# Splitting a weight unit in one pass instead of two on GpSimd

## The reference

```python
proj = xn @ w_in                 # 1024 x 3072, 1024 x 5632, 2816 x 1024, ...
x = x + (b * u) @ w_out
x = x + (jax.nn.silu(a) * g) @ w_down
...
merged = jax.nn.sigmoid(gate_a) * y_gla + jax.nn.sigmoid(gate_b) * y_swa
x = x + merged @ w_out[l]
```

## Time and profile before

| | |
|---|---|
| median of 3 runs | 2173.0 us (2172.61 to 2173.7) |
| the profiled execution | 2173.7 us, its span 2171.9 us |
| TensorE matmul busy (PE) | 98% of the span |
| GpSimd busy (POOL) | 69% |
| VectorE busy (DVE) | 45% |
| ScalarE busy (ACT) | 20% |
| instructions of GpSimd | 1615 |
| bytes moved | 193.44 MB, mean 89 GB/s |
| mean granted TensorE clock | 0.997 of full |

### The profile page before, as it was taken

How to read it: one execution, slowest core, us unless ns; L and a number is a source line. 1 busy time by engine, 2 the same in 40 slices (tenths; PEclk the granted TensorE clock), 3 DMA queues, 4 the chain that set the end, 5 groups by cost and what they waited for, 6 DMA issues and landing times.

```text
span 2171.9 us, 30026 instructions
## 1 busy us (share of the span) xinstructions
PE 2122.8 (98%) x10839; PEld 1771.5 (82%) x10847; DVE 981.3 (45%) x1527; ACT 428.9 (20%) x871; POOL 1503.2 (69%) x1615
## 2 busy tenths in 40 slices
PE   5999999999999999999999999999999999999999
PEld 4888888888798887888888888888877888888887
DVE  5555655531446666675541156345744243222201
ACT  2002111100334434211100053222223112111000
POOL 4878888867764445798877846445544777777674
PEclk9999999999999999999999999999999999999999
DMA  4333333323333221333323322223222333333232
GB/s 125 97 106 107 90 96 96 93 81 99 104 103 83 78 78 49 103 107 98 96 75 97 112 75 70 77 59 88 59 72 65 88 98 97 97 97 97 80 90 82
DMA packets 366903, 193.44 MB, mean 89 GB/s; under 512 B 6512, under 2 KB 363216, under 8 KB 366816
## 3 DMA queue, kind: packets, MB, share of 16 engines
q1 hardware_dynamic: 363168, 186.67, 30.1%
q10 hardware_dynamic: 3648, 5.59, 0.8%
HBM read 190.11 MB, written 2.13 MB: 89 GB/s over the span
## 4 chain that ended last, share of the span: by engine, by line
PE 93%; DVE 4%; ACT 1%; issue 1%; ACTq 0%; DMA 0%; DVEq 0%
PE PS L482 22%; PE PS L484 22%; PE PS L483 22%; PE PS L745 2%; PE PS L729 2%; PE PS L630 2%; PE PS L731 2%; PE PS L730 2%; PE PS L746 2%; PE PS L747 2%; PE PS L632 2%; PE PS L631 2%; PE PS L546 1%; PE PS L577 1%; PE PS L814 1%; PE PS L952 1%
## 5 line engine op out<-in xcount | busy, mean ns | idle before, releaser
L465 POOL TENSOR_TENSOR RING<-RAW,RING 128x512 fp32r<-128x512 f32 x708 | 966.2, 1365 | 59.0
L462 POOL TENSOR_SCALAR RING<-RAW 128x512 fp32r<-128x512 f32 x708 | 514.5, 727 | 429.1 <-PE PS L747 110.8
L482 PE MATMUL PS<-XH,RING 128*128 128x512 f32 x1344 | 526.4, 392 | 4.4 <-DVE XT L2138 2.6
L483 PE MATMUL PS<-XL,RING 128*128 128x512 f32 x1344 | 523.9, 390 | 0.0
L484 PE MATMUL PS<-XH,RING 128*128 128x512 f32 x1344 | 523.7, 390 | 0.0
L482 PEld LDWEIGHTS PS<-XH,RING 128*128 128x128 f32 x1344 | 253.0, 188 | 59.1 <-DVE XT L2138 3.0
L483 PEld LDWEIGHTS PS<-XL,RING 128*128 128x128 f32 x1344 | 252.9, 188 | 53.6 <-issue 1.2
L484 PEld LDWEIGHTS PS<-XH,RING 128*128 128x128 f32 x1344 | 252.8, 188 | 52.7
L482 PE MATMUL PS<-HH,RING 128*128 128x512 f32 x528 | 205.4, 389 | 0.0
L483 PE MATMUL PS<-HL,RING 128*128 128x512 f32 x528 | 205.4, 389 | 0.0
L484 PE MATMUL PS<-HH,RING 128*128 128x512 f32 x528 | 205.4, 389 | 0.0
(11 more groups left out here) (298 smaller groups left out, 3332.1 us busy)
## 6 DMA issues: line engine op xcount, KB each, us to landing
RAW<-in_ffn_w_up SPq DMA_DIRECT2D x88, 512.0 KB, 3.7
RAW<-in_w_in SPq DMA_DIRECT2D x53, 512.0 KB, 3.7
RAW<-in_w_ffn_in SPq DMA_DIRECT2D x44, 512.0 KB, 3.8
RAW<-in_ffn_w_down SPq DMA_DIRECT2D x32, 512.0 KB, 3.9
RAW<-in_a_w_in SPq DMA_DIRECT2D x24, 512.0 KB, 3.6
RAW<-in_w_kvf SPq DMA_DIRECT2D x17, 512.0 KB, 3.9
RAW<-in_b_w_qg SPq DMA_DIRECT2D x16, 512.0 KB, 3.7
RAW<-in_w_ffn_out SPq DMA_DIRECT2D x16, 512.0 KB, 3.7
```

What stands on the lines that cost most here:

```text
L462: hi = pool.tensor_scalar(WH[s][:, k0_:k1, :], RAW[s][:, k0_:k1, :], 1.0, 1.0, ALU.mult, ALU.mult)
L465: lo = pool.tensor_tensor(WL[s][:, k0_:k1, :], RAW[s][:, k0_:k1, :], WH[s][:, k0_:k1, :].bitcast(F32), ALU.subtract)
L482: pe.matmul(o, WH[s][:, k, :], xh[:, k0 + k, :], start=first and k == 0, stop=False)
L483: pe.matmul(o, WH[s][:, k, :], xl[:, k0 + k, :], start=False, stop=False)
```

## The change

The four instructions of a unit become two. The high part of all row blocks is written by one `tensor_scalar` and the low part by one `tensor_tensor`. `high_done` counts once for each unit. `split_done` is raised once for each unit as before, by the last instruction. Nothing changes on another engine.

```diff
-                        for h, (k0_, k1) in enumerate(((0, 4), (4, nk))):
-                            hi = pool.tensor_scalar(WH[s][:, k0_:k1, :], RAW[s][:, k0_:k1, :], 1.0, 1.0, ALU.mult, ALU.mult)
-                            hi.then_inc(high_done, 1)
-                            pool.wait_ge(high_done, p.unit(i, j) * 2 + (h + 1))
-                            lo = pool.tensor_tensor(WL[s][:, k0_:k1, :], RAW[s][:, k0_:k1, :],
-                                                    WH[s][:, k0_:k1, :].bitcast(F32), ALU.subtract)
-                            if h:
-                                lo.then_inc(split_done, 1)
+                        pool.tensor_scalar(WH[s][:, 0:nk, :], RAW[s][:, 0:nk, :], 1.0, 1.0, ALU.mult, ALU.mult).then_inc(high_done, 1)
+                        pool.wait_ge(high_done, p.unit(i, j) + 1)
+                        pool.tensor_tensor(WL[s][:, 0:nk, :], RAW[s][:, 0:nk, :], WH[s][:, 0:nk, :].bitcast(F32),
+                                           ALU.subtract).then_inc(split_done, 1)
```

## The result

The change made the kernel slower. The median is 2186.7 us (2185.1 to 2187.1) where the kernel before took 2173.35 beside it: a ratio of 1.0058, with a 95% interval of 1.0043 to 1.0075, or 13.3 us. The forecast was 7 us: 2180.0, with 2177 to 2184 as its own range and 2172 to 2187 as the outer one. So the loss is nearly twice the forecast, and the time lies at the upper end of the outer range. The profiled execution's span is 2184.5 us, 12.6 longer than before.

A forecast was written before the change was run, and what follows sets the result against it. TensorE was taken as the bound, waiting at few places for DVE, which longer POOL instructions shut out; 5 + 1.0 + 1.4 - 1.0 + 0.4 + 0.5 = 7.3, taken as 7, gave 2180.0 us (2177 to 2184; outer 2172 to 2187).

The forecast's parts named there:

- much slower: Rival, chance 0.12: merged low part takes 2.52 us, GLA and SWA chains come bare too; twice the sum, 2187.
- line through the two sizes: POOL's merged instructions, extrapolated from those of 256 and 512 numbers: 1.06 us high part, 2.32 us low part.
- SWA: TensorE's wait for L1950 near 1561 to 1575 grows as DVE is shut out longer: 5 us.
- worse walk: SWA stretch if L1983 or L1989 comes just behind a POOL instruction: the chain ends 6.2 us later.
- Start of attention: 574 to 591: L1699 ends later, L1530 meets a longer low part; TensorE's wait at L665 grows 1.0 (0 to 2.5).
- QN: Attention: second QN chunk late, new wait of 1.0 before L630, 0.2 in each later copy; 1.4 (0 to 3).
- OF: Attention, three times: the burst ends sooner and the wait before L608 shrinks by about 0.35; -1.0 (-1.5 to 0).
- Elsewhere: Entries into the feed-forward blocks, one GLA output and the attention output: about +0.4 us (0 to 2).
- Clock: After the SWA wait, a longer wait may move or draw out the clock drop: 0.5 (-1.5 to +2).
- should hardly fall or rise: DVE's busy time over the kernel: nearly unchanged, as its waits are fewer and longer.
- Nothing that can be measured: Rival, chance 0.30: DVE shut out longer here, shorter there, hidden by TensorE's reserve; 2172 to 2177, say 2175.
- Faster: Rival, chance 0.08: every burst ends sooner, 0.4 us a unit; 5.7 us gained, 2167.3.

The follow-up runs named there:

- e1: The changed kernel with halves again for the 12 units of merge1 alone; 2179.9 us, ratio 1.0025.
- e2: The kernel before with one pass for the 12 units of merge1 alone; 2180.3 us, ratio 1.0022.
- e4: The changed kernel, with GpSimd held before merge1's unit 2 until the last XN is written; 2176.8 us, ratio 1.0011.
- e3: The kernel before with one pass in the ten hardware-loop phases alone, 252 of 354 units; 2177.1 us, ratio 1.0009.
- e8: The kernel before, with GpSimd held before merge1's unit 2 until the last XN is written; 2172.5 us, ratio 0.9987.
- e6: Against the kernel before, the high part in one instruction and the low part still in two halves, everywhere; 2179.8 us, ratio 1.0021.
- e7: Against the kernel before, every unit in quarters instead of halves; 2198.5 us, ratio 1.0108.
- e9: Against the kernel before, quarters everywhere but in the input products of the first two feed-forward blocks, which keep halves; 2162.3 us, ratio 0.9947.

## Why the prediction was right, and where it was short

As a whole, the direction, the place and the mechanism were forecast, the size was not. 13.3 us were measured for 7. The time lies above the forecast's own range (2177 to 2184) and at 2186.7 almost on the number of the rival "much slower" (2187), which had a chance of 0.12. That rival was half right: its longer low part didn't come, its bare GLA chain did.

**What bounds the kernel.** Right but for a detail. TensorE is the bound, and the change acts almost only through DVE. "No row there names POOL" holds for the view, but the wait of 0.34 us before the first `w_o_gla` unit was for POOL, and its going was worth 0.65 us.

**The durations.** The line through the two sizes gave 1.06 and 2.32; the trace has 1.04 and 2.34. The upper bound of 1.24 and 2.52 was not touched. The 0.45 us for each unit that GpSimd saves are there (POOL 1503 to 1283 us, partly the turns that DVE no longer takes) and were worth nothing, but for those 0.65 us.

**SWA, 5.** Right in mechanism and nearly in size: 5.9, of which the wait is 6.5 and the sooner first unit -0.65. The worse walk, with L1942 waiting for another low part, gave 6.2 for the wait. It let L1983 or L1989 slip; after the change both met an instruction (L1979 and L1985 there). e1 and e2 show the place, e4 the cause. By the Trainium skill (SBUF — State Buffer, "Who interferes with whom") the ports that VectorE and GpSimd share are an exclusive lock held for the whole instruction; e4's 1.41 in place of 6.96 us agrees. By the same section of the Trainium skill TensorE never waits for anyone's port. No wait here speaks against that, but it didn't make the loss nil: TensorE waited 10.2 us for the engine that does wait.

**Start of attention, 1.0; QN, 1.4; OF, -1.0.** 1.1, 1.2 and -0.8. The three OF waits shrank from 0.66, 0.66 and 0.74 to 0.35, 0.36 and 0.45 as forecast. The wait at L626 is 0.69, forecast 1.0; the later copies have no wait that the view shows, only steps of about 0.15.

**Elsewhere, +0.4.** This is the term that failed. It was given as 0.4 (0 to 2) and measured 3.7: 1.2 at the entry into the second feed-forward block, 1.3 at L786 for YGL, 0.5 at the attention output, 0.4 in the last block, 0.3 in the first. The small ones are no scatter: the last block and the first have the same steps to 0.1 us in e1, e3 and e4. The prediction named these places, one GLA output among them, and shows no walk for them. The rival gave the GLA chain a reserve of 4 us and more. One scan there, L1776, started 0.5 us behind a low part and takes 3.28 us where its work is 1.22; it waited 1.0 before the change and 2.1 after it, and the reserve was gone:

```profile
1339.48 3.28 DVE L1776 TENSOR_TENSOR_SCAN BC<-RESET,ZC 128x512 f32<-128x512 f32 x1
...
1343.60 1.41 DVE L1852 SCALAR_TENSOR_TENSOR YGL<-PS,PRM,YGH 128x512 fp32r<-128x512 f32 x2 [0.83 <-ACT YGH L1359]
```

The bare GLA chain stood in the rival "much slower" as part of the worst, and should have been in the sum with its price. The 0.6 in the opening is within what unchanged stretches show (0.5 and 0.8 in e8 and e2).

**Clock, 0.5.** The sum is 0.6, and that is luck. Behind the SWA wait, where the prediction looked for it, the clock cost 0.2 us less than before (0.79 for 0.77). The rest came behind the unchanged wait for KTT: from 1285 to 1320 the clock is 0.90 after and 0.95 before, and the table steps by 0.85. The same step comes in e2, whose code there is that of before, with a clock of 0.90, and none in e6 and e8, with 0.95. So it isn't the change's: the clock is worth a microsecond or so at a wait of some 4 us, with either sign.

**DVE's busy time "should hardly fall or rise".** Wrong by 186 us. I reasoned from bursts with a fixed total. In the hardware loops DVE comes back in every unit at the same point of POOL's work, as L1559 does 0.24 us behind the low part, and waits for the rest of it. e3 has 163 of the 186 us and costs about 2 us.

**The rivals.** "Nothing that can be measured" fell with the SWA wait; e3 is what it would have looked like. "Faster" needed the chain to end behind the burst; in SWA four instructions were inside it. "Much slower" gave the time and half of the reason, as said above.

The measured terms in the order of the prediction's sum, then the opening and what no term holds: 5.9 + 1.1 + 1.2 - 0.8 + 3.7 + 0.6 + 0.6 + 0.3 = 12.6. Beside 5 + 1.0 + 1.4 - 1.0 + 0.4 + 0.5, "elsewhere" alone makes 3.3 of the 5.3 us that were missing.

## What to carry to other kernels

Merging instructions on GpSimd saves its own time, which is worth something only where another engine waits for it; what it lengthens is how long VectorE can be shut out. Cut it fine where a VectorE chain is bare (quarters gave 11.5 us here) and coarser where GpSimd then has no room left (here the two stretches with the convolution, where quarters cost 18 us each), and where a burst isn't needed at once, let it wait for the chain. To find the places, don't look at VectorE's busy time: match the same matmuls of two traces and see where the distance steps.

## What the runs showed of the hardware that was not expected

- A VectorE instruction on 128x4 numbers with two inputs waits as long as a large one: 2.15 us for a work of 0.16 (e4 and after). The reciprocal of the same tile, with one input, did not wait beside a running high part (0.18 us at 1574.77 in after).
- The wait is not smooth. With the same GpSimd burst, met 0.01 us later by the first instruction of the chain (before and e3), the wait for XN was 3.7 and 5.6 us.
- GpSimd gets slower too where VectorE takes turns: a low part of a quarter took 1.05 in place of 0.73 us in e7 while DVE had L1587 and L1590 to do (1.10 us at 203.43, 0.88 at 204.46).

```profile
204.88 1.05 POOL L488 TENSOR_TENSOR RING<-RAW,RING 128x256 fp32r<-128x256 f32 x1
...
206.39 0.73 POOL L488 TENSOR_TENSOR RING<-RAW,RING 128x256 fp32r<-128x256 f32 x1
```

- In e9 TensorE has no wait for TINY, and in SWA one of 1.1 and one of 0.6 us in place of 3.7. The granted clock stays at 1.00 from 575 to 600 and from 1565 to 1605, where before it was 0.93 and 0.91. Removing the long waits gave back the slow stretches behind them as well.
